# Experts of a decoder trunk: weights as the loaded operand, blocks of 96 token rows streamed beside their rests

## The chip, the cores and the metric

The kernel runs on one core of a Trainium2 chip. The metric is the device time of one execution in microseconds (us). TensorE (PE in the profile, with its weight loads as PEld), VectorE (DVE), ScalarE (ACT), GpSimd (POOL) and the DMA queue of SyncE (SP) run side by side and are ordered by semaphores alone.

## The reference, cut to what matters

One inference step of a two-layer trunk for 256 prompt rows and 32 sample rows (T = 288), width D = 1024. Layer 0 is a Mamba and attention mixer with a dense SwiGLU; layer 1 is RWKV-7 time mixing and a mixture of 8 experts, of which each row goes to 2. The change is in the experts:

```python
def _swiglu(h, wg, wu, wd):
    return (jax.nn.silu(h @ wg) * (h @ wu)) @ wd
...
    logits = jnp.einsum('bld,de->ble', h.astype(f32), router.astype(f32))
    top_v, top_i = lax.top_k(logits, TOP_K)
    gates = jax.nn.softmax(top_v, axis=-1)
...
    for e in range(N_EXPERTS):
        y = y + combine[..., e:e + 1] * _swiglu(h, wg[e], wu[e], wd[e]).astype(f32)
```

`wg` and `wu` are 1024 x 2816 and `wd` is 2816 x 1024 for each expert, in float32: 34.6 MB an expert.

## The kernel before, in words

Every expert product is made in fp32r, a faster 32-bit form of TensorE with fewer mantissa bits. To keep the precision each operand is split in a head (the value rounded to fp32r) and a rest (value less head, rounded), and three products are added: head by head, head by rest, rest by head. For the weights ACT makes the heads (`heads`, lines 1411 to 1423) and DVE the rests (`rests`, lines 2138 to 2150).

Token rows are first grouped: each expert's rows go into a block of 128 slots, and an expert with more rows than slots gets a further block. A block is a *job*. DVE works out the number of jobs on the chip (`jobf`, `jobi`, `jobs_ready`); the engines run job 0, a loop over the middle jobs and the last job, which is expert 7. Job 0's rows are picked by matmuls; those of later jobs come from a DRAM scratch `moe_rows`, fetched by POOL (`next_rows`) and turned by TensorE into `hsel` (`turn_tokens`, line 3080). After a job ACT copies the result to `ysb` (`rows_out`), and POOL stores it in `moe_back` (`store_rows`, waiting for the landing). In the last job the rows of the other experts are gathered (`pair`, `DMA_INDIRECT`), scaled, turned (`pair_turn`) and added to `x`; the last expert's own rows are put back by a matmul with `sel_last`.

In a job the 2816 hidden units go in FC = 11 chunks of 256. SP loads a chunk's weights in two DMAs, gate and up (2 MB, "gu") and down (1 MB, "dn"), into one of MS = 4 slots; a slot's part is loaded again when its matmuls are done (`gu_slot_free`, `dn_slot_free`). TensorE's order in a job is written out by hand:

```python
                for c in range(FC + 2):
                    if c < FC:
                        up(c)
                    if c >= 2:
                        down(c - 2)
                    if 1 <= c < FC:
                        turn(c - 1)
```

`up(c)` makes gate and up of 256 units for 128 token rows in one PSUM bank. For each of 8 k tiles the token columns are loaded and 512 weight columns are streamed, three times (every matmul is issued in the helper at line 2342):

```python
                        mm(ps[:, c % 2, :], hh[:, k, :], wh[:, k, :], k == 0, False)
                        mm(ps[:, c % 2, :], hh[:, k, :], wr[:, k, :], False, False)
                        ins = mm(ps[:, c % 2, :], hr[:, k, :], wh[:, k, :], False, k == KT - 1)
```

Then ACT takes silu of the gate half (line 1486), DVE multiplies by the up half (line 2291), TensorE turns the product by two transposes (`turn`, line 3127), ACT makes its head (line 1493) and DVE its rest (line 2307). `down(c)` loads these (128 units by 128 rows) and streams 512 columns of the down weights, 12 matmuls. One chunk's heads and rests are in the queues of ACT and DVE between these steps, two chunks ahead of TensorE.

Of the kernel before, what the change touches and what calls it, by code (L numbers as in the profile page):

```python
# [32 lines left out]
FC = FF // 256  # L33
C_DECAY = float(np.exp(-0.5))
# [95 lines left out]
def decoder_trunk(nc, a, out):  # L130
    with ExitStack() as ctx:
# [216 lines left out]
        sgm = moe_area(256)  # L348
        actm = [moe_area(256) for _ in range(2)]

        actTm = [[actTm_[:, (2 * i + u) * 256:(2 * i + u + 1) * 256] for u in range(2)] for i in range(2)]
# [6 lines left out]
        NJ = NE + 4  # L358
        flags, posn, erow, jrow = [moe_area(16) for _ in range(4)]
        ohx, tmpx = [moe_area(64).rearrange("p (x i) -> p x i", x=4) for _ in range(2)]  # L360
# [11 lines left out]
        DOWN_BANKS = [0, 1, 2, 7, 5, 6, 3, 4]  # L372
        moe_rows = nc.dram_tensor("moe_rows", ((NJ + 1) * P, D), F32, kind="Internal").ap()
        moe_back = nc.dram_tensor("moe_back", (NJ * P, D), F32, kind="Internal").ap()

# [13 lines left out]
        def turned(c):  # L389

            return ps[:, 2 if c % 2 == 0 else 7, 0:256]
# [368 lines left out]
        def _(sp):  # L760
# [110 lines left out]
            jl = sp.value_load(jobi[0:1, 4:5], min_val=NE - 1, max_val=NJ - 1)  # L871
# [12 lines left out]
        def _(pool):  # L884
# [15 lines left out]
            for n, t in enumerate(X_ORDER):  # L900
# [11 lines left out]
                if n == 4:  # L912
                    pool.wait_ge(sem("pool_cleared"), 2)
                    pool.dma_start(moe_rows.rearrange("(b p) n -> p b n", p=P), zeros.unsqueeze(1).broadcast_to([P, NJ + 1, D]))\
                        .then_inc(sem("rows_zeroed"), 16)
                    pool.dma_start(moe_back[(NE - 1) * P:, :].rearrange("(b p) n -> p b n", p=P),
                                   zeros.unsqueeze(1).broadcast_to([P, NJ - NE + 1, D])).then_inc(sem("rows_zeroed"), 16)
# [91 lines left out]
            jl = pool.value_load(jobi[0:1, 4:5], min_val=NE - 1, max_val=NJ - 1)  # L1009
            def next_rows(j):  # L1010
                pool.wait_ge(sem("gather_full"), 2 * j + 2)
                pool.dma_start(xtok, moe_rows[bass.ds(j * P + P, P), :]).then_inc(sem("xtok_loaded"), 16)
# [7 lines left out]
            next_rows(0)  # L1020
            with pool.Fori(1, jl) as j:
                next_rows(j)
                store_rows(j)
            pool.wait_ge(sem("gather_full"), 2 * jl + 2)
            store_rows(jl)
            for c, (t0, n) in enumerate(TOK):
                if c == 2:
                    pool.wait_ge(sem("pair_summed"), 1)
                    pool.wait_ge(sem("y_final"), 2)
                for a_ in range(2):  # L1030
                    pool.indirect_dma_start(pair[a_][c][0:n, :], None, moe_back,
                                            bass.IndirectOffsetOnAxis(ap=rows_in[0:n, 3 * a_ + c:3 * a_ + c + 1], axis=0))\
                        .then_inc(sem(f"pair_loaded{c}"), 16)


        @block.scalar
        def _(act):
# [387 lines left out]
            def token_heads(j, u):  # L1425

                act.wait_ge(sem("gather_full"), 2 * j + 1 + u)
                A(hsel[0][:, 4 * u:4 * u + 4, :], ps[:, 5 + u, :].rearrange("p (k c) -> p k c", k=4), ACT.Copy)\
                    .then_inc(sem("hsel_head"), 1)

            def rows_out(j):
# [3 lines left out]
                A(ysb[:, 0:512], ps[:, 3, :], ACT.Copy)  # L1435
                A(ysb[:, 512:1024], ps[:, 4, :], ACT.Copy).then_inc(sem("y_out"), 1)
# [29 lines left out]
            def job(j, first, last=False):  # L1466
# [4 lines left out]
                else:  # L1471
                    heads(j, 0, "gu", range(4))
                    rows_out(j)
                    heads(j, 1, "gu", range(2))
                for c in range(FC + 1):
# [858 lines left out]
        def _(pe):  # L2334
# [748 lines left out]
            def job(j, opening, last=False):  # L3083
# [67 lines left out]
                for c in range(FC + 2):  # L3151
# [4 lines left out]
                    if 1 <= c < FC:  # L3156
                        turn(c - 1)
# [125 lines left out]
```

## Time and profile before

| | |
|---|---|
| median of 3 runs | 1634.34 us (1631.61 to 1641.16) |
| profiled execution | 1637.31 us |
| its span, first to last instruction | 1634.3 us |
| mean granted TensorE clock, share of 2.4 GHz | 0.987 |
| PE, PEld, DVE, ACT, POOL busy, share of the span | 97%, 80%, 70%, 55%, 8% |

All stretches and waits below are of the profiled execution. Busy time of an engine is the time that at least one of its instructions is running; matmuls are pipelined, so a matmul's own duration is longer than the distance to the next one. A granted clock of 1.00 is 2.4 GHz, 0.50 is 1.2 GHz. The experts begin at about 850 us; before that come the mixers and the dense layer.

### The profile page before, as it was taken

The page shows a single profiled execution, that of the slowest core. Times are in us where ns is not written, and L with a number is a line of the kernel's source. Part 1 is how long each engine was busy: PE and PEld are TensorE (multiplying, and loading weights), DVE is VectorE, ACT ScalarE, POOL GpSimd, SP SyncE. Part 2 cuts the span into 40 slices and gives each one's busy share as a digit, 9 for nine tenths or more (in the row PEclk, how much of TensorE's full clock was granted, in tenths as well). Part 3 has the DMA queues.
Part 4 walks back from the last instruction along what each step waited for, and adds up shares of the span by engine and source line. Part 5 has one row for each costly group of instructions (what it writes and reads, how often), then busy time and mean ns, then how long its engine had stood idle before and what let it go on. Part 6 is the DMA issues. An engine that isn't in the chain of part 4 may idle for free.

```text
span 1634.3 us, 27320 instructions
## 1 busy us (share of the span) xinstructions
PE 1590.1 (97%) x10856; PEld 1309.2 (80%) x10856; DVE 1137.9 (70%) x1476; ACT 896.8 (55%) x1190; POOL 123.3 (8%) x180
## 2 busy tenths in 40 slices
PE   9999999999999999899999999999999999999999
PEld 7766687999998777778767878888787887878787
DVE  4663741677766753335468889797988979798897
ACT  3362541544325353343436777676777767687774
POOL 1104000000000003220222000000000000000100
PEclk9999889999999999998999999999999999999999
DMA  8923533544423240000449999797989979798993
GB/s 334 407 94 124 207 130 123 220 187 170 175 81 119 103 155 1 3 3 2 187 165 395 380 376 412 316 427 305 425 350 376 409 312 426 303 425 347 384 423 121
DMA packets 41103, 404.74 MB, mean 248 GB/s; under 512 B 4784, under 2 KB 5072, under 8 KB 11664
## 3 DMA queue, kind: packets, MB, share of 16 engines
q1 hardware_dynamic: 34336, 372.25, 56.6%
q0 software_dynamic: 6672, 31.14, 4.7%
q8 instruction: 70, 1.15, 0.3%
q14 instruction: 25, 0.20, 0.0%
HBM read 379.09 MB, written 26.30 MB: 248 GB/s over the span
## 4 chain that ended last, share of the span: by engine, by line
PE 88%; DVE 5%; ACT 2%; DMA 2%; issue 2%; POOL 0%; DVEq 0%; ACTq 0%; SPq 0%; POOLq 0%
PE ps L2342 85%; DMA ring<-in_moe_w 1%; PE ps L3127 1%; DMA arena<-in_moe_w 1%; DVE rest_ring L2149 1%; PE ps L2809 1%; PE ps L2750 1%; DVE arena L1688 0%; ACT arena L1270 0%; DVE arena L1701 0%; ACT arena L1283 0%; PE ps L3080 0%; PE ps L2544 0%; DVE h L2057 0%; DVE arena L1776 0%
## 5 line engine op out<-in xcount | busy, mean ns | idle before, releaser
L2342 PE MATMUL ps<-head,hsel 128*128 128x512 f32 x1408 | 457.5, 396 | 2.8 <-DVE rest_ring L2149 2.8
L2342 PEld LDWEIGHTS ps<-head,hsel 128*128 128x128 f32 x1408 | 264.3, 188 | 61.5 <-DVE rest_ring L2149 7.8
L2149 DVE TENSOR_TENSOR rest_ring<-ring,head 128x2048 fp32r<-128x2048 f32 x128 | 291.0, 2284 | 14.4 <-ACT head L1423 14.3
L2342 PE MATMUL ps<-arena,ring 128*128 128x288 f32 (+9 forms) x1408 | 256.6, 347 | 1.3 <-ACT arena L1276 1.2
L1423 ACT ACTIVATE head<-ring 128x2048 fp32r<-128x2048 f32 x128 | 243.1, 1912 | 24.9 <-DMA ring<-in_moe_w 24.9
L2342 PEld LDWEIGHTS ps<-arena,ring 128*128 128x128 f32 (+4 forms) x1408 | 199.5, 189 | 53.1 <-issue 7.7
L2342 PE MATMUL ps<-rest_ring,hsel 128*128 128x512 f32 x512 | 199.6, 390 | 0.0
L2342 PE MATMUL ps<-head,actT_split 128*128 128x512 f32 x512 | 169.1, 394 | 9.0 <-issue 6.3
L2342 PE MATMUL ps<-rest_arena,head 128*128 128x288 f32 x704 | 174.8, 296 | 0.0
L2342 PE MATMUL ps<-rest_arena,rest_ring 128*128 128x288 f32 x528 | 155.5, 294 | 0.0
L2342 PE MATMUL ps<-h,ring 128*128 128x288 f32 (+2 forms) x624 | 133.6, 370 | 3.7 <-ACT h L1332 1.9
L2342 PEld LDWEIGHTS ps<-h,ring 128*128 128x128 f32 (+2 forms) x624 | 99.6, 176 | 37.6 <-issue 10.7
L2342 PEld LDWEIGHTS ps<-head,actT_split 128*128 128x128 f32 x512 | 96.1, 188 | 33.3 <-issue 9.1
L2342 PEld LDWEIGHTS ps<-rest_arena,head 128*128 128x128 f32 x704 | 122.5, 188 | 0.1
L2143 DVE TENSOR_TENSOR rest_ring<-ring,head 128x2048 fp32r<-128x2048 f32 x48 | 109.7, 2285 | 9.7 <-ACT head L1418 9.7
L2149 DVE TENSOR_TENSOR rest_arena<-arena,head 128x1024 fp32r<-128x1024 f32 (+1 forms) x64 | 110.3, 1750 | 3.7 <-ACT head L1423 3.5
L2342 PEld LDWEIGHTS ps<-rest_ring,hsel 128*128 128x128 f32 x512 | 96.4, 188 | 18.0
L2342 PE MATMUL ps<-arena 64*64 64x64 f32 (+13 forms) x1514 | 96.9, 266 | 9.9 <-DVE arena L1721 4.0
L2342 PE MATMUL ps<-hsel,head 128*128 128x288 f32 x352 | 103.8, 295 | 0.0
L1599 DVE TENSOR_TENSOR x<-x,ps 128x288 f32<-128x288 f32 x110 | 48.2, 452 | 77.6 <-PE ps L2342 77.3
L1423 ACT ACTIVATE head<-arena 128x1024 fp32r<-128x1024 f32 (+1 forms) x64 | 92.4, 1485 | 15.9 <-DMA arena<-in_moe_w 15.6
L2342 PE MATMUL ps<-rest_ring,actT_split 128*128 128x512 f32 x256 | 99.7, 389 | 0.0
(387 smaller groups left out, 2283.1 us busy)
## 6 DMA issues: line engine op xcount, KB each, us to landing
ring<-in_moe_w SPq DMA_DIRECT2D x64, 2048.0 KB, 12.4
ring<-in_moe_w SPq DMA_DIRECT2D x64, 1024.0 KB, 8.3
arena<-in_moe_w SPq DMA_DIRECT2D x24, 2048.0 KB, 11.6
arena<-in_moe_w SPq DMA_DIRECT2D x24, 1024.0 KB, 6.6
ring<-in_ffn_w SPq DMA_DIRECT2D x11, 2048.0 KB, 7.4
ring<-in_ffn_w SPq DMA_DIRECT2D x11, 1024.0 KB, 4.8
moe_rows<-arena POOLq DMA_DIRECT2D x1, 6656.0 KB, 34.0
ring<-in_w_in SPq DMA_DIRECT2D x2, 3072.0 KB, 12.8
```

The costliest lines, as they stand in the source:

```text
L1423: A(mhead[c % 2][:, o:o + w], mslot[s][:, o:o + w], ACT.Copy).then_inc(sem("gu_head"), 1)
L1599: V.tensor_tensor(x[:, m, :], x[:, m, :], bank(g)[:, 0:T], ALU.add).then_inc(freesem(g), 1)
L2143: V.tensor_tensor(mrest[s][:, GU:SLOT], mslot[s][:, GU:SLOT], down_head(c).bitcast(F32), ALU.subtract).then_inc(sem("dn_split"), 1)
L2149: V.tensor_tensor(mrest[s][:, o:o + w], mslot[s][:, o:o + w], mhead[c % 2][:, o:o + w].bitcast(F32), ALU.subtract).then_inc(sem("gu_split" ...
L2342: return nc.tensor.matmul(o, l, r, start=start, stop=stop, skip_group_check=skip)
L2750: ins = nc.tensor.transpose(b[0:rows, i * P:(i + 1) * P], src[:, 4 * hf + i, t0:t0 + rows], ident)
L2809: ins = nc.tensor.transpose(b[:, n * P:(n + 1) * P], Mi[gg % 2][:, h0:h0 + 2, :].rearrange("p h t -> p (h t)"), ident)
L3127: ins = nc.tensor.transpose(turned(c)[:, u * P:(u + 1) * P], actm[c % 2][:, u * P:(u + 1) * P], ident)
```

## The change

- Blocks have 96 slots (`SL`), not 128; thresholds, row numbers, scratch tensors and the number of possible further blocks (5, not 4) follow.
- In `up` the weights are the loaded operand and token rows are streamed. Head and rest of the token rows stand beside each other in `hsel` (192 columns), so head by head and rest by head are one matmul; the third, with the rests of the weights, streams the 96 head columns. 64 matmuls a chunk. The result has hidden units on partitions: two banks, in each two 128-unit blocks with (head columns, rest columns).
- The two parts are summed: ACT copies the rest columns (`gsum`), DVE adds the head columns (`act_sums`). Then silu (ACT, now from SBUF), product (POOL), head (ACT), rest (POOL). `turn` is gone; the token transposes have 96 columns.
- POOL's queue now has, per job, the products and rests of 11 chunks (`activations`), and between them the store of the last job's rows (after chunk 0), the wait for its landing (after chunk 1), and in the last job the gathers (after chunks 1 and 7).
- `down` loads 96 columns in place of 128. PSUM banks: 0 and 1, 2 and 3 for gate and up; 4 and 5 for down; 6 and 7 for token rows. ACT makes the first head piece of the next job before its last activation head.

```diff
+SL = 96
-        hsel = [hsel_[:, i * 1024:(i + 1) * 1024].rearrange("p (k c) -> p k c", k=KT) for i in range(2)]
+        hsel = hsel_[:, 0:2 * KT * SL].rearrange("p (k a c) -> p k a c", k=KT, a=2)
-        NJ = NE + 4
+        NJ = NE + 5
...
+        def gu_banks(c):
+
+            b = GU_BANKS[c % 2]
+            return ps[:, b:b + 2, 0:4 * SL].rearrange("p b (i a s) -> p b i a s", i=2, a=2)
...
-            def store_rows(j):
-                pool.wait_ge(sem("y_out"), j)
-                pool.dma_start(moe_back[bass.ds(j * P - P, P), :], ysb).then_inc(sem("back_stored"), 16)
-                pool.wait_ge(sem("back_stored"), 16 * j)
-                pool.sem_inc(sem("ysb_free"), 1)
+            def activations(j, first, c):
+
+                if c or not first:
+                    pool.wait_ge(sem("moe_act_rest"), FC * j + c)
+                pool.wait_ge(sem("sums_then_silu"), 2 * FC * j + 2 * c + 2)
+                nc.gpsimd.tensor_tensor(actm, sgm[c % 2], gsum[c % 2][:, 2 * SL:4 * SL], ALU.mult).then_inc(sem("actm_ready"), 1)
+                pool.wait_ge(sem("moe_act_head"), FC * j + c + 1)
+                nc.gpsimd.tensor_tensor(actTm[c % 2][1], actm, actTm[c % 2][0].bitcast(F32), ALU.subtract)\
+                    .then_inc(sem("moe_act_rest"), 1)
+            def job(j, first, last=False):
+                if not last:
+                    next_rows(j)
+                for c in range(FC):
+                    activations(j, first, c)
+                    if c == 0 and not first:
+                        pool.wait_ge(sem("y_out"), j)
+                        pool.dma_start(moe_back[bass.ds(j * SL - SL, SL), :], ysb[0:SL]).then_inc(sem("back_stored"), 16)
+                    if c == 1 and not first:
+                        pool.wait_ge(sem("back_stored"), 16 * j)
+                        pool.wait_ge(sem("gather_full"), 2 * j + 2)
+                        pool.sem_inc(sem("ysb_free"), 1)
+                    if last and c == 1:
+                        pair_rows(0)
+                        pair_rows(1)
...
+            def act_silu(j, c):
+
+                act.wait_ge(sem("gu_free"), FC * j + c + 3)
+                A(sgm[c % 2], gsum[c % 2][:, 0:2 * SL], ACT.Silu).then_inc(sem("sums_then_silu"), 1)
+            def act_head(j, c):
+
+                act.wait_ge(sem("actm_ready"), FC * j + c + 1)
+                if c >= 2:
+                    act.wait_ge(sem(f"dn_slot_free{(c - 2) % MS}"), uses[(c - 2) % MS] * j + (c - 2) // MS + 2)
+                A(actTm[c % 2][0], actm, ACT.Copy).then_inc(sem("moe_act_head"), 1)
...
+                    A(sums4(c), gu_banks(c)[:, :, :, 1, :], ACT.Copy).then_inc(sem("sums_then_silu"), 1)
...
+                    act_silu(j, c)
                     if c + 2 < FC:
                         heads(j, c + 2, "gu", range(1, 2))
+                    if c == FC - 1 and not last:
+                        heads(j + 1, 0, "gu", range(0, 1))
+                    act_head(j, c)
...
+            def act_sums(j, c):
+
+                dve.wait_ge(sem("sums_then_silu"), 2 * FC * j + 2 * c + 1)
+                V.tensor_tensor(sums4(c), gu_banks(c)[:, :, :, 0, :], sums4(c), ALU.add).then_inc(sem("gu_free"), 1)
...
-                        mm(ps[:, c % 2, :], hh[:, k, :], wh[:, k, :], k == 0, False)
-                        mm(ps[:, c % 2, :], hh[:, k, :], wr[:, k, :], False, False)
-                        ins = mm(ps[:, c % 2, :], hr[:, k, :], wh[:, k, :], False, k == KT - 1)
+                        for i in range(4):
+                            cols_ = slice(i * P, (i + 1) * P)
+                            both = sums[:, i // 2, i % 2]
+                            if k == KT - 1:
+                                mm(both[:, 0], wr[:, k, cols_], hsel[:, k, 0, :], False, False, skip=True)
+                            ins = mm(both, wh[:, k, cols_], hsel[:, k], k == 0 and i % 2 == 0, k == KT - 1, skip=True)
+                            if k < KT - 1:
+                                mm(both[:, 0], wr[:, k, cols_], hsel[:, k, 0, :], False, False, skip=True)
...
-                    for u in range(2):
-                        ins = nc.tensor.transpose(turned(c)[:, u * P:(u + 1) * P], actm[c % 2][:, u * P:(u + 1) * P], ident)
...
-                        mm(ps[:, 3 + hf, :], ah[:, us], wh[:, u, cols_], begins, False)
+                        mm(ps[0:SL, DOWN + hf, :], ah[:, us], wh[:, u, cols_], begins, False)
```

## Rows read from the trace of the kernel before

**Rows 1.** The page: busy us (share of the span) x instructions; costliest group.
```profile
PE 1590.1 (97%) x10856; PEld 1309.2 (80%) x10856; DVE 1137.9 (70%) x1476; ACT 896.8 (55%) x1190; POOL 123.3 (8%) x180
...
L2342 PE MATMUL ps<-head,hsel 128*128 128x512 f32 x1408 | 457.5, 396 | 2.8 <-DVE rest_ring L2149 2.8
```

**Rows 2.** The chain of waits that ended last, shares of the span by engine.
```profile
PE 88%; DVE 5%; ACT 2%; DMA 2%; issue 2%; POOL 0%; DVEq 0%; ACTq 0%; SPq 0%; POOLq 0%
```

**Rows 3.** Two stretches: us, PE, PEld, DVE, ACT, POOL busy (x), PEclk, DMA share, GB/s.
```profile
949.39:1044.96 95.57, 94.41 (x427) 76.93 (x428) 82.53 (x60) 70.24 (x62) 1.10 (x2) 1.00 0.91 374
...
1523.32:1634.27 110.95, 106.32 (x485) 85.91 (x485) 96.56 (x86) 73.61 (x66) 12.12 (x7) 1.00 0.75 310
```

**Rows 4.** The chain in order of time, one job's end and start: start, us, what.
```profile
1235.16 0.87 PE ps L3080 x8
...
1259.04 1.58 issue
...
1263.63 0.22 PE ps L3127 x2
1263.85 8.17 PE ps L2342 x36
...
1280.66 8.20 PE ps L2342 x36
```

**Rows 5.** Timeline at a job's start, TensorE idle before: start us, us, engine, line.
```profile
1154.72 0.19 PEld L2342 LDWEIGHTS ps<-head,hsel 128*128 128x128 f32 x1 [0.82 <-DVE rest_ring L2149]
1154.72 0.50 PE L2342 MATMUL ps<-head,hsel 128*128 128x512 f32 x1 [0.40 <-DVE rest_ring L2149]
1154.83 0.19 PEld L2342 LDWEIGHTS ps<-rest_ring,hsel 128*128 128x128 f32 x1
1155.06 0.40 PE L2342 MATMUL ps<-rest_ring,hsel 128*128 128x512 f32 x1
```

**Rows 6.** Timeline, weight loads in the time mixer, plain fp32, 64 columns streamed each.
```profile
776.62 0.86 PEld L2342 LDWEIGHTS ps<-arena,ring 128*128 128x128 f32 x7 [0.24 <-issue]
```

**Rows 7.** Timeline, fp32r matmuls of 288 columns in the dense layer.
```profile
442.83 0.29 PE L2342 MATMUL ps<-rest_arena,rest_ring 128*128 128x288 f32 x1
442.96 0.42 PE L2342 MATMUL ps<-rest_arena,head 128*128 128x288 f32 x2
```

**Rows 8.** Groups by form, six jobs (949.39 to 1523.32): busy us, mean ns, idle before.
```profile
L2149 DVE TENSOR_TENSOR rest_ring<-ring,head 128x2048 fp32r<-128x2048 f32 x96 | 218.2, 2284 | 3.7 <-ACT head L1423 3.6
L2342 PEld LDWEIGHTS ps<-head,hsel 128*128 128x128 f32 x1056 | 198.2, 188 | 46.9 <-DVE rest_ring L2149 6.7
L1423 ACT ACTIVATE head<-ring 128x2048 fp32r<-128x2048 f32 x96 | 182.3, 1912 | 10.8 <-DMA ring<-in_moe_w 10.8
...
L2149 DVE TENSOR_TENSOR rest_arena<-arena,head 128x1024 fp32r<-128x1024 f32 x24 | 27.7, 1217 | 0.0
L2291 DVE TENSOR_TENSOR moe<-moe,ps 128x256 f32<-128x256 f32 x66 | 27.7, 419 | 51.2 <-ACT moe L1486 51.1
...
L1486 ACT ACTIVATE moe<-ps 128x256 f32<-128x256 f32 x66 | 25.3, 384 | 90.2 <-PE ps L2342 90.2
...
L3127 PEld LDWEIGHTS ps<-cst,moe 128*128 128x128 f32 x132 | 18.0, 139 | 7.8
...
L2156 DVE TENSOR_TENSOR hsel<-ps,hsel 128x512 fp32r<-128x512 f32 x12 | 7.7, 682 | 0.0
```

**Rows 9.** One line of POOL, both operands in SBUF: duration ns min/median/max.
```profile
L954 POOL TENSOR_TENSOR ring<-ring,cst x40: 632/635/1180, 629.1 to 738.2; 128x256 f32<-128x256 f32 x40
```

**Rows 10.** One line of DVE, both operands in SBUF: duration ns min/median/max.
```profile
L1543 DVE TENSOR_TENSOR arena<-arena x21: 451/452/736, 271.3 to 842.8; 128x288 f32<-128x288 f32 x21
```

**Rows 11.** Busy time in a stretch of the time mixer (columns as in rows 3).
```profile
640.00:660.00 20.00, 16.68 (x448) 13.15 (x446) 8.82 (x17) 13.13 (x32) 4.57 (x8) 1.00 0.01 3
```

**Rows 12.** DMA issues in six jobs: KB each, median us from issue to landing.
```profile
moe_back<-moe POOLq DMA_DIRECT2D x6, 512.0 KB, 10.2
```

More of the change, by code:

```diff
@@ L357, in decoder_trunk @@
         rows_in = moe_area(6).bitcast(U32)
-        NJ = NE + 4
+        NJ = NE + 5
         flags, posn, erow, jrow = [moe_area(16) for _ in range(4)]
-        ohx, tmpx = [moe_area(64).rearrange("p (x i) -> p x i", x=4) for _ in range(2)]
+        ohx, tmpx = [moe_area(80).rearrange("p (x i) -> p x i", x=5) for _ in range(2)]
         rk = moe_area(32)
@@ L1033, in _ @@
                         .then_inc(sem(f"pair_loaded{c}"), 16)
+            def job(j, first, last=False):
[13 more added lines that the diff above has]
+                        pair_rows(1)
+                    if last and c == 7:
+                        pool.wait_ge(sem("pair_summed"), 1)
+                        pool.wait_ge(sem("y_final"), 2)
+                        pair_rows(2)
+            job(0, True)
+            with pool.Fori(1, jl) as j:
+                job(j, False)
+            job(jl, False, last=True)
         @block.scalar
@@ L2284, in job @@
                     rests(j, 0, "gu", range(4))
-                    rests(j, 1, "gu", range(0, 1))
-                for c in range(FC + 1):
-                    if c < FC:
-                        dve.wait_ge(sem("silu_ready"), FC * j + c + 1)
-                        if c >= 2:
-                            dve.wait_ge(sem("tr_full"), FC * j + c - 1)
-                        V.tensor_tensor(actm[c % 2], sgm, ps[:, c % 2, 256:512], ALU.mult).then_inc(sem("gu_free"), 1)
+                    rests(j, 1, "gu", range(2))
+                for c in range(FC):
+                    act_sums(j, c)
                     if last and c in (2, 3):
@@ L2297, in job @@
                         pair_add(j, c // 2 - 3, c % 2)
-                    if c == 0 and not first:
-                        rests(j, 1, "gu", range(1, 2))
-                    if 1 <= c <= FC - 2:
+                    if c:
                         rests(j, c - 1, "dn", range(1))
                     if c + 2 < FC:
-                        rests(j, c + 2, "gu", range(0, 1))
-                    if c:
-                        dve.wait_ge(sem("tr_head"), FC * j + c)
-                        hd = actTm[(c - 1) % 2]
-                        V.tensor_tensor(hd[1], turned(c - 1), hd[0].bitcast(F32), ALU.subtract).then_inc(sem("tr_free"), 1)
-                    if c + 2 < FC:
-                        rests(j, c + 2, "gu", range(1, 2))
-                    if c == FC - 2:
-                        rests(j, c, "dn", range(1))
+                        rests(j, c + 2, "gu", range(2))
                 rests(j, FC - 1, "dn", range(1))
```

154 lines of the change are left out of this document (67 added, 87 removed).

## The prediction

> **What bounds the kernel now.** I read the page's busy times first: PE is busy 97% of the span, DVE 70%, ACT 55%, POOL 8%, and the experts' gate and up matmuls are the costliest group, 1408 records; they are two of the three matmuls of each k tile, so one job has 11 x 8 x 2 = 176 of them and there are 8 jobs [rows 1]. The chain of waits gives PE 88% [rows 2]. Busy PE is no proof of peak speed, so I went to the stretch by job: a full job takes 95.6 us, PE is busy for 94.4 of it at granted clock 1.00, DVE 82.5, ACT 70.2, DMA engines 91% of the time; the last one takes 110.95 with its tail [rows 3]. The chain inside a job then says what the job is made of: 36 matmuls in 8.17 to 8.20 us, two transposes in 0.22 us, eleven times; eight transposes of token rows in 0.87 us once; and a few short waits at the job's start [rows 4]. So one matmul of 512 streamed columns costs 8.20 / 36 = 0.228 us from start to start. 512 columns at 2.4 GHz are 0.213 us. TensorE's order of work sets the end and the other engines follow: whatever changes TensorE's time for one chunk is paid 88 times.
>
> The jobs stay eight. A block of 96 rows would need a further job for each expert with over 96 rows, but the reference's router, evaluated on the reference's inputs, gives the eight experts 70, 77, 68, 84, 76, 64, 60 and 77 rows.
>
> **The change part by part.**
>
> *Gate and up matmuls.* Before, a chunk of 256 hidden units takes 8 k tiles x 3 matmuls = 24, each loading 128 token columns and streaming 512 weight columns: 24 x 0.228 = 5.47 us. After, the weights are loaded: 8 k tiles x 4 column blocks x 2 = 64 matmuls, each loading 128 x 128, half of them streaming 192 columns (heads beside rests) and half 96. By columns that is 32 x (192 + 96) = 9216 in place of 12288. If only columns counted, this would be a gain. So the question is what a weight load costs when little is streamed behind it.
>
> The trace answers twice. When TensorE has been idle and an fp32r matmul starts, its load starts at 1154.72, the next load at 1154.83 and the second matmul at 1155.06 [rows 5]: 0.34 us from first to second start in place of 0.228. The extra 0.11 is the first load standing alone, and the next load begins when it is over. So a 128 x 128 fp32r load takes 0.11 us before its matmul can stream; with 512 columns behind it that is hidden. The second place has loads of 128 columns with only 64 streamed: seven loads in 0.86 us, and the last one's own record is 0.19, so starts are (0.86 - 0.19) / 6 = 0.112 us apart [rows 6]. These are plain fp32, which streams each column twice: the streaming alone would be 0.053. There the load is the bound, at clock 1.00 as in the experts.
>
> 192 columns are 0.080 us and 96 are 0.040, both under 0.11, so all 64 starts should be a load apart. No row shows fp32r with few streamed columns. Bounds: below, 0.108, the bare load of rows 5; above, 0.120, since fp32r matmuls have a fixed part over their columns that plain ones lack (288 columns, 0.120 us, start 0.13 apart [rows 7]; 512 have 0.015), which might add to the load. I take 0.112, the row that is bound in the same way. Up costs 64 x 0.112 = 7.17 us (6.91 to 7.68), 1.70 more.
>
> Here a page speaks otherwise. The Trainium skill, TensorE: Matmul & The Clock Gate, section Back-to-back issue gap, gives about 81 ns for each sustained pair of load and 128-column matmul. By it up would be 64 x 0.081 = 5.18 us, a gain; no run here shows 0.081, and rows 5 and 6 show more, so I don't use it in the sum.
>
> *Transposes of activations.* They go: two per chunk, 0.22 us [rows 4]. Gate and up now come out with hidden units on partitions.
>
> *Down matmuls.* 12 per chunk, 512 streamed, as before: 12 x 0.228 = 2.74. Their load has 96 columns, hidden as 128 were. Token transposes: at most the same 0.87 per job.
>
> *A chunk.* Before 8.20 + 0.22 = 8.42 (11 of them and 0.87 leave 2.1 of a job of 95.6 for waits). After 7.17 + 2.74 = 9.91, 1.49 more.
>
> *The evacuation chain.* It now has six steps: ACT copies the products with token rests (384 elements), DVE adds, ACT silu (192), POOL multiplies, ACT makes the head, POOL the rest. The old steps took 0.38 to 0.42 us for 256 elements and 0.68 (DVE) for 512 [rows 8], so 384 on DVE is 0.55. ACT per chunk: three heads of 1.91, plus about 0.5, 0.3 and 0.3: 6.8 us. DVE: three rests of 2.28 plus 0.55: 7.4 us, against 7.7 before. POOL: two operations of some 0.6 us (635 ns for 256 elements, with one operand broadcast [rows 9]; here 192). All below 9.91: hidden. down(c) stands after up(c+2), 2 x (7.17 + 2.74) = 19.8 us behind up(c)'s end, and the chain with two heads of ACT work between needs about 6 to 8. At the job's end down(10) follows up(10) by down(8), the token transposes and down(9), 6.3 us: nearly tight, since POOL's two steps can each stand behind one of DVE's 2.28 us instructions.
>
> *POOL against DVE.* POOL's operation of 635 ns takes up to 1180, DVE's of 452 up to 736 [rows 9, 10], each with both operands in SBUF and where the other engine works on SBUF too. So DVE may lose 2 x 0.28 to 2 x 0.54 us a chunk: 8.0 to 8.5. Still under 9.91; with a faster TensorE it would not be.
>
> *Moved waits.* POOL's store of rows and its landing (10.2 us [rows 12]) now stand between its products at c = 0 and c = 1; next in its queue are the products of chunk 2, which ACT's head waits for, and behind that ACT's heads of weights. down(2) starts 19.8 us after up(2), so nothing is late. In the last job four indirect gathers stand there too; the same slack covers them if they hold POOL for under some 10 us. Loads from DRAM: same bytes at a slower pace, 91% of 95.6 in 110. Their queue waits for slots freed by the same matmuls. What is left at a job's start is the DVE piece for up(0); I leave 0.5 us of waits, because pieces of 1.22 us on DVE now feed 1.79 us of matmuls.
>
> *Sum.* A job: 11 x 9.91 + 0.87 + 0.5 = 110.4, against 95.6: 14.8 more, x 8 = 118. The last job's PE idles 4.6 us against 1.2 in a full one [rows 3]; those 3.4 should vanish, as weights come early enough now. +115. Router, mixers and dense layer are untouched. The profiled execution took 1637.31 us (span 1634.3); with the change 1752. The median of the runs is 1634.34: 1749.
>
> **Rivals.**
>
> *Loads are cheaper than that and columns count (faster).* The place is the same 64 matmuls. For it: transposes' loads of 128 columns have a record of 139 ns where the fp32r ones have 188 [rows 8]. If the load took 49 ns less, 192 columns would cost 0.093 and 96 some 0.054 to 0.067: up 4.7 to 5.15, a chunk 7.4 to 7.9, and then DVE at 8.0 to 8.5 becomes the bound. Job 89 to 94.5, mid value 91: 4.6 x 8 = 37 less, 1597. It decides when the mean interval is under (8.42 - 2.74) / 64 = 0.089 us. Against it: the 0.11 of rows 5 is on fp32r loads themselves. The Trainium skill, SBUF — State Buffer, section Who interferes with whom, says that a two-SBUF-input DVE instruction and a POOL one that reads SBUF exclude each other; by this rule the gain would stop at DVE as reckoned, and the trace agrees (452 to 736 ns, rows 10).
>
> *The load isn't hidden at all when streams are short:* 0.108 + 0.080 and 0.108 + 0.040, with fixed parts about 0.17 on average: up 10.9, chunk 13.6, +5.2 x 88 = +458, less 12 of waits: 2080. Against it: in rows 6 load and stream overlap (0.112, not 0.16).
>
> *The granted clock falls to 1.2 GHz in the experts,* since TensorE streams only half of the time there. A chunk doubles to 19.8: +1000, 2630. Against it: the stretch of small products with PE gaps of 17% stays at 1.00 [rows 11].
>
> **How the numbers follow.** Load bound, slower: 0.83. Cheaper loads: 0.08. Unhidden loads 0.04, clock 0.03, other 0.02. Time 1749, the likeliest. Its range: interval 0.108 gives -23, 0.120 gives +45; waits of 0 to 2.5 a job give -4 to +16; the last job's stall kept +3. That is 1722 to 1813; I trim the corner where all are high and take 1718 to 1805, which leaves out the rivals. Faster by over 0.5% 0.08, within 0.5% (what a measurement of this kernel can't tell from none) 0.01, slower 0.91.
>
> **What the profile after would show.** PE's expert matmuls of 192 and 96 columns start 0.108 to 0.120 us apart whatever their width; PEld is then continuous; up about 7.2 us, chunk about 9.9, job about 110; DVE and ACT each idle 1.5 to 3 us a chunk; DMA share near 0.8; clock 1.00. I am wrong if the two widths differ in interval (loads not the bound), if DVE rests or POOL products end TensorE's waits, if a granted clock of 0.5 stands in the expert stretch, or if there are more than eight jobs.

## The result, and the profile after

The median went from 1633.47 us (1631.61 to 1641.16) to 1898.15 us (1896.36 to 1899.15): ratio 1.161, 95% interval 1.158 to 1.165. Forecast were 1749 us and 1718 to 1805. The direction and the first mechanism were right, but the forecast is 149 us low.

The page after; columns as in [rows 1, 2]:

```profile
PE 1841.3 (97%) x14200; PEld 1617.9 (85%) x14200; DVE 1172.5 (62%) x1388; ACT 918.6 (48%) x1278; POOL 383.9 (20%) x356
...
PE 85%; DVE 6%; issue 5%; ACT 2%; POOL 1%; DMA 0%; DVEq 0%; POOLq 0%; ACTq 0%
...
L2373 PE MATMUL ps<-hsel,head 128*128 128x192 f32 (+1 forms) x3168 | 855.1, 345 | 18.4 <-issue 18.3
L2190 DVE TENSOR_TENSOR rest_ring<-ring,head 128x2048 fp32r<-128x2048 f32 x128 | 327.7, 2599 | 14.6 <-ACT head L1454 14.6
```

PE is as busy as before, 97%. That alone would pass for "TensorE does more work". The issue share in front of the new matmuls (18.3 us) is the first hint that something else has come in. Then the stretches by job, with the columns of [rows 3]: job 1 up to its last downs, the first 44 us of job 2, and the rest of job 2:

```profile
988.49:1092.82 104.33, 104.23 (x821) 96.71 (x820) 81.25 (x44) 67.39 (x66) 31.92 (x22) 1.00 0.82 321
1102.90:1147.20 44.30, 44.13 (x200) 42.84 (x199) 18.05 (x11) 15.83 (x16) 8.13 (x6) 0.50 0.57 223
1147.20:1236.00 88.80, 87.04 (x645) 77.69 (x644) 66.66 (x38) 55.60 (x55) 25.57 (x19) 1.00 0.73 281
```

PE is busy in all three, but in the second at granted clock 0.50 (1.2 GHz), with 200 matmuls in 44 us. Six such stretches stand in the experts, one at the opening of each of jobs 0 and 2 to 6; jobs 1 and 7 have none. The weight loads of up, at full clock and then in such a stretch (timeline, PEld):

```profile
1150.02 0.19 PEld L2373 LDWEIGHTS ps<-hsel,rest_ring 128*128 128x128 f32 x1
1150.13 0.19 PEld L2373 LDWEIGHTS ps<-hsel,head 128*128 128x128 f32 x1
1150.24 0.19 PEld L2373 LDWEIGHTS ps<-hsel,rest_ring 128*128 128x128 f32 x1
```

```profile
1110.08 0.33 PEld L2373 LDWEIGHTS ps<-hsel,head 128*128 128x128 f32 x1
1110.29 0.33 PEld L2373 LDWEIGHTS ps<-hsel,rest_arena 128*128 128x128 f32 x1
```

They start 0.111 us apart at full clock and 0.21 at half, the same for both widths. The starts of the matmuls themselves alternate (timeline, PE):

```profile
1149.73 0.32 PE L2373 MATMUL ps<-hsel,head 128*128 128x192 f32 x1
1149.88 0.23 PE L2373 MATMUL ps<-hsel,rest_ring 128*128 128x96 f32 x1
1149.95 0.32 PE L2373 MATMUL ps<-hsel,head 128*128 128x192 f32 x1
```

The next one starts 0.156 us behind one of 192 columns and 0.067 behind one of 96. Taken by itself that is a sign of being wrong that the prediction names (the two widths differ), but a pair always takes 0.223 us, two loads, so the pace is that of the loads. At full clock up takes 7.12 us, down 2.78, a chunk 9.90. Last, the end of job 2 and the start of job 3 (timeline; DVE's first weight rests, PE's last down, PE's first up):

```profile
1231.67 4.62 DVE L2190 TENSOR_TENSOR rest_arena<-arena,head 128x1024 fp32r<-128x1024 f32 x4
...
1233.95 0.40 PE L2373 MATMUL ps<-head,actT_split 128*96 128x512 f32 x1
...
1237.92 0.35 PE L2373 MATMUL ps<-hsel,head 128*128 128x192 f32 x1 [3.57 <-issue]
```

The first of the four rests was done at 1232.9, both pieces of hsel before it. No engine's work is late here, and yet for 3.57 us TensorE runs nothing. The trace's record of its branch at the end of the loop's body begins at 1231.5 and lasts 6.04 us. The five branches that go back take 5.9 to 6.3 us, and 0.22 to 0.24 in the kernel before; the sixth, which leaves the loop, 0.08. The instruction queue q8 moved 125 packets (2.05 MB), against 70 (1.15 MB): TensorE's body has 844 matmuls, each with a load, in place of 426.

So my account of the miss, from the starts of matmuls: from down(9) to the next up(0) five times 3.8 us more than in jobs that follow no branch (19 us); and the three opening ups at 41.0 to 41.3 us in place of 21.4, with the first down at 3.5 to 5.0 in place of 2.8, six times (127 us). Together 146. (The experts take 147 us more than the sum said, as counted below; the small rest of the 149 lies ahead of them.)

### The profile page after: what moved, and what is told of

It reads as the page before. It is cut to its first block, busy times and chain, and to the rows that moved or that the text cites. A ratio compares the mean times of both kernels' runs of the same rounds, so it can differ in the third digit from the quotient of the medians.

```text
span 1894.7 us, 34341 instructions
## 1 busy us (share of the span) xinstructions
PE 1841.3 (97%) x14200; PEld 1617.9 (85%) x14200; DVE 1172.5 (62%) x1388; ACT 918.6 (48%) x1278; POOL 383.9 (20%) x356
## 3 DMA queue, kind: packets, MB, share of 16 engines
q8 instruction: 125, 2.05, 0.4%
## 4 chain that ended last, share of the span: by engine, by line
PE 85%; DVE 6%; issue 5%; ACT 2%; POOL 1%; DMA 0%; DVEq 0%; POOLq 0%; ACTq 0%
PE ps L2373 84%; DVE rest_ring L2184 1%; DVE rest_arena L2190 1%; PE ps L2840 1%; POOL moe L1028 1%; DMA moe_back<-moe 0%; PE ps L2781 0%; DVE arena L1729 0%; ACT arena L1301 0%; DVE arena L1742 0%; ACT arena L1314 0%; PE ps L2575 0%; DVE h L2098 0%; DVE arena L1817 0%; POOL actT_split L1030 0%
## 5 line engine op out<-in xcount | busy, mean ns | idle before, releaser
L2373 PE MATMUL ps<-hsel,head 128*128 128x192 f32 (+1 forms) x3168 | 855.1, 345 | 18.4 <-issue 18.3
L2373 PEld LDWEIGHTS ps<-hsel,head 128*128 128x128 f32 x3168 | 684.0, 216 | 25.3 <-issue 20.8
L2373 PE MATMUL ps<-hsel,rest_ring 128*128 128x96 f32 x2048 | 493.4, 251 | 0.0
L2373 PEld LDWEIGHTS ps<-hsel,rest_ring 128*128 128x128 f32 x2048 | 441.6, 218 | 2.1
L2190 DVE TENSOR_TENSOR rest_ring<-ring,head 128x2048 fp32r<-128x2048 f32 x128 | 327.7, 2599 | 14.6 <-ACT head L1454 14.6
L1028 POOL TENSOR_TENSOR moe<-moe 128x192 f32<-128x192 f32 x88 | 125.4, 1425 | 637.3 <-ACT moe L1472 637.3
L2373 PE MATMUL ps<-hsel,rest_arena 128*128 128x96 f32 x768 | 189.5, 257 | 1.7 <-issue 1.7
L2373 PE MATMUL ps<-head,actT_split 128*96 128x512 f32 x512 | 178.0, 410 | 1.4 <-DVE rest_ring L2184 0.7
L2373 PEld LDWEIGHTS ps<-hsel,rest_arena 128*128 128x128 f32 x768 | 170.5, 225 | 3.1 <-issue 2.4
L1030 POOL TENSOR_TENSOR actT_split<-moe,actT_split 128x192 fp32r<-128x192 f32 x88 | 142.6, 1621 | 70.5 <-ACT actT_split L1479 70.5
L2373 PEld LDWEIGHTS ps<-h,ring 128*128 128x128 f32 (+2 forms) x624 | 99.5, 176 | 37.4 <-issue 10.5
L2373 PEld LDWEIGHTS ps<-head,actT_split 128*96 128x96 f32 x512 | 86.6, 169 | 39.9 <-POOL actT_split L1030 3.5
```

What stands on the lines that cost most here:

```text
L1028: nc.gpsimd.tensor_tensor(actm, sgm[c % 2], gsum[c % 2][:, 2 * SL:4 * SL], ALU.mult).then_inc(sem("actm_ready"), 1)
L1030: nc.gpsimd.tensor_tensor(actTm[c % 2][1], actm, actTm[c % 2][0].bitcast(F32), ALU.subtract)\
L2190: V.tensor_tensor(mrest[s][:, o:o + w], mslot[s][:, o:o + w], mhead[c % 2][:, o:o + w].bitcast(F32), ALU.subtract).then_inc(sem("gu_split" ...
L2373: return nc.tensor.matmul(o, l, r, start=start, stop=stop, skip_group_check=skip)
```

## The experiments

The theory: the branch leaves TensorE idle, the granted clock falls, and three ups with thin streams in a row don't bring it back; the first wide matmuls (down(0)) do. Rivals: thin streams alone bring it down; the idle time comes from DVE or GpSimd; the fall has a length of its own.

Times up to job 0's first up differ by up to 13 us between runs of kernels that are alike there (852 to 865 us), so beside each median stands the *experts' part*, from the start of that matmul to the end in the profiled execution: 776.0 us before, 1037.5 after. The prediction's sum was 776 + 115 = 891. "On e1" means that the edit is made in the first experiment's kernel, which has no branch on TensorE between jobs; its time is 1771 us.

**TensorE's middle jobs written out.** (e1)

```diff
-            with pe.Fori(1, jl) as j:
+            for j in range(1, NE - 1):
                 job(j, False)
```

> TensorE's middle jobs of the changed kernel are written out one after the other in place of its loop; every other engine keeps its loop. Theory (an idle time of TensorE at the loop's branch lets the granted clock fall, and the three ups that follow without a down hold it down): the five idle times of 3.8 us go (19 us), and with them the falls at the openings of jobs 2 to 6 (21.2 us each, 106); the fall in job 0, which has no branch before it, stays. 1898 - 19 - 106 = 1773 us. Rival 1 (thin streams alone bring the clock down wherever three ups follow each other): only the idle times go, 1879. Rival 2 (the idle time is not the branch but late pieces from DVE or POOL): no change, 1898.

Measured 1771.45 us, ratio 1.082 (1.077 to 1.088); experts' part 912.5. One row of windows, the three opening ups of job 2:

```profile
1093.11:1114.52 21.41, 21.41 (x193) 21.41 (x192) 18.27 (x11) 15.91 (x16) 7.85 (x5) 1.00 1.00 394
```

No idle time, clock 1.00, 21.4 us. Three thin ups in a row don't bring the clock down by themselves (rival 1 would be 1879). Five of the six falls went with the branch; job 0's stayed.

**The idle time put back without a branch** (on e1; e5)

```diff
                 if not first:
+                    for n_ in range(2):
+                        V.reduce_sum(tmpx[:, n_, 0:KT], x, AX)
                     rests(j, 0, "gu", range(4))
```

> The kernel of the run with TensorE's jobs written out (1771 us), with DVE made late: before its first weight rest of each job but the first it sums all of x twice (about 2.4 us each, result not used), so that up(0) waits some 3.4 us for DVE (2 to 5) although there is no branch. Theory (any idle time of TensorE in front of three thin ups brings the clock down, the branch is only one maker of it): falls of about 44 us at the openings of jobs 1 to 7, 21 us each: 1771 + 7 x (3.4 + 21) = 1942 us. Rival (the fall needs what comes with the branch, such as the fetch of instructions): no falls, 1771 + 7 x 3.4 = 1795 us.

Measured 1945.03 us, ratio 1.184 (1.179 to 1.189); experts' part 1079.8. DVE and PE at the start of job 3 (timeline), and that opening (windows):

```profile
1259.02 5.00 DVE L2330 TENSOR_REDUCE moe<-x 128x8 f32<-128x2304 f32 x2
1263.94 4.61 DVE L2190 TENSOR_TENSOR rest_arena<-arena,head 128x1024 fp32r<-128x1024 f32 x4
...
1265.25 0.33 PE L2375 MATMUL ps<-hsel,head 128*128 128x192 f32 x1 [3.58 <-issue]
```

```profile
1265.25:1305.68 40.43, 40.43 (x192) 40.43 (x193) 21.11 (x12) 12.90 (x12) 7.82 (x5) 0.51 0.64 247
```

The view calls this idle time issue too, though here it ends when DVE's first piece does: the label alone tells no cause. All seven openings behind such a wait now run at half clock, those of jobs 1 and 7 as well. An idle time of 3.6 us was enough here; the branch is only what made it in the changed kernel.

**The branch moved in front of down(9) and down(10)** (loop kept; e6; down(9)'s waits for its operands move to the end of the body, ahead of the branch)

```diff
             def job(j, opening, last=False):
...
+                if not opening:
+                    down(FC - 2, True)
+                    down(FC - 1, True)
-                for c in range(FC + 2):
+                for c in range(FC + 2 if last else FC):
```

> The changed kernel with its loop, but the turn of the loop on TensorE is moved: down(9) and down(10) of a job stand after the branch, ahead of the next job's up(0). Instructions and their order on every engine are the same. Theory: the idle time at the branch stays (five times 3.8 us), but 24 wide matmuls follow it, so the clock is back before the three ups; falls of some 3.4 us as in the kernel before with two jobs a turn, under 2 us each; job 0 keeps its fall. 1771 + 19 + 8 = 1798 us. Rival (an idle time brings a long fall whatever follows): 1898.

Measured 1823.7 us, ratio 1.111 (1.106 to 1.117); experts' part 959.5, 47 more than in e1. The first matmul behind the branch, and the windows of the two downs and of the three ups behind them:

```profile
1217.75 0.71 PE L2373 MATMUL ps<-head,actT_split 128*96 128x512 f32 x1 [7.11 <-issue]
```

```profile
1217.75:1225.89 8.14, 8.14 (x24) 5.48 (x25) 5.33 (x3) 0.98 (x1) 0.00 (x0) 0.66 0.56 168
1225.89:1247.31 21.42, 21.42 (x193) 21.41 (x192) 11.78 (x7) 13.88 (x14) 7.85 (x5) 1.00 0.97 387
```

The clock fell here too, but the wide streams brought it back within the two downs, which took 8.1 us in place of 5.8, and the ups ran at full clock. So what follows the idle time sets the price: 2.3 us or 21. I was 26 us low. The idle time grew from 3.8 us to 6.9 to 7.1, 15 us in five turns; the downs lost 4 us more than I had counted; the other 7 us are within what the stages ahead of the experts vary by. In the loop as it was, the 12 queued matmuls of down(10) ran on for 2.8 us behind the branch's start; here only eight short transposes stood in front of the branch.

**12 wide matmuls inside up(0) and up(1)** (loop kept; e2)

```diff
+                        if k == KT - 1 and c < 2:
+                            for n_ in range(12):
+                                mm(ps[0:SL, TOKB + n_ % 2, :], hsel[:, n_ % 8, 0, :], wh[:, n_ % 8, :])
                         for i in range(4):
```

> The changed kernel, loop kept, with 12 matmuls of 512 columns into banks that nobody reads before the last k tile of up(0) and of up(1) in every job. At full clock they cost 2 x 2.74 = 5.5 us a job. Theory (the clock comes back once wide streams run, whatever they compute): up(0) still runs at half clock, and the clock comes back within the first wide matmuls, so an affected opening costs about 7 + 2 us in place of 21; 1898 - 6 x 12 + 8 x 5.5 = 1870 us. Rival (the fall has a fixed length of some 44 us whatever TensorE streams): 12 wide ones at half clock cost 5.5 each time, 11 a job; 1898 + 6 x 11 + 2 x 5.5 = 1975. The idle time at the branch stays at 3.8 us in both.

Measured 1885.1 us, ratio 1.150 (1.144 to 1.156); experts' part 1022.3. The falls are shorter (windows at job 3: up(0) with its wide matmuls, then what follows):

```profile
1236.40:1256.90 20.50, 15.79 (x65) 14.56 (x66) 2.34 (x2) 0.00 (x0) 0.00 (x0) 0.50 0.52 207
1256.90:1275.60 18.70, 18.70 (x152) 17.59 (x151) 11.77 (x7) 12.92 (x12) 7.84 (x5) 1.00 0.78 300
```

The fall has no length of its own (1975 is excluded): it ended with the wide matmuls of up(0). The falls cost 6.2 to 7.6 us an opening (26.9 us at full clock), less than the 9 I had counted. The gain is smaller than expected for another reason: behind each branch TensorE stands still a second time, in up(0) after five matmuls (timeline):

```profile
1237.22 0.49 PE L2373 MATMUL ps<-hsel,head 128*128 128x192 f32 x1
1242.41 0.24 PE L2373 MATMUL ps<-hsel,rest_arena 128*128 128x96 f32 x1 [4.70 <-issue]
```

These five idle times of 4.6 to 5.4 us, 25 us together, have no match in the other runs; in the one shown DVE's four pieces for up(0) had ended at 1234.3. The edit makes TensorE's body longer (868 matmuls), but why it stops there is not shown.

**The kernel before, two jobs in each turn of TensorE's loop** (e3)

```diff
-            with pe.Fori(1, jl) as j:
-                job(j, False)
+            with pe.Fori(0, NE // 2 - 1) as i_:
+                job(2 * i_ + 1, False)
+                job(2 * i_ + 2, False)
```

> The kernel before, with two jobs in each turn of TensorE's loop (three turns in place of six), so that the loop's body has about as many instructions (some 850 matmuls) as the changed kernel's body has. Theory (a taken branch costs TensorE some 6 us once the body is this long, whatever the streams; and wide streams bring the clock back soon): two back edges with a branch of about 6 us and an idle time of 3 to 4 us, three job starts without a branch; a clock fall, if any, of under 6 us each. 1634 + 2 x 3 - 3 x 1.6 = 1635 us, up to 1645 with short clock falls. Rival (the long branch comes from narrow matmuls or from the other engines' state in the changed kernel, not from the body's length): branches stay at about 0.2 us, 1629 to 1634.

Measured 1651.05 us, ratio 1.010 (1.003 to 1.017); experts' part 791.3, 15.3 more. That is over my 1635 to 1645 us, and well over the rival's 1629 to 1634. Its two branches back take 6.7 and 6.2 us. The first matmul behind one (timeline) and the opening ups (windows):

```profile
1153.50 0.64 PE L2342 MATMUL ps<-head,hsel 128*128 128x512 f32 x1 [4.08 <-issue]
```

```profile
1153.50:1167.02 13.52, 12.95 (x48) 10.13 (x49) 6.74 (x5) 6.43 (x5) 0.00 (x0) 0.87 1.01 423
```

The long branch comes from the length of the body, not from the new matmuls. The clock fell here as well, and cost 1.8 us (13.5 in place of 11.75) with 512 columns streamed at once. About the same idle time costs some 20 us with thin streams. The two branches and their falls make 11.5 of the 15.3 us; the rest are longer waits in front of the first down of some jobs and changes too small to place. Behind one of these, of 1.8 us and without a branch, the clock fell too, for 3.4 us (windows, job 2's up(2) and down(0)):

```profile
1063.11:1074.95 11.84, 10.01 (x40) 7.67 (x39) 10.91 (x8) 8.01 (x7) 0.00 (x0) 0.87 1.02 434
```

Behind an idle time of 1.9 us that ended at 974.0 in the same run it didn't fall. So no least idle time for a fall can be read from these runs.

**The kernel before, TensorE's jobs written out** (the edit of e1; e4)

> The kernel before with TensorE's middle jobs written out in place of its loop. Theory: the idle 1.58 us marked as issue at each of five back edges goes, 8 us: 1626 us. Rival (what TensorE waits for there is DVE's first piece, so the branch is covered): 1634.

Measured 1637.01 us, ratio 1.002 (0.999 to 1.006): no change, the rival's time. The branch of 0.23 us was covered, and the waits marked issue [rows 4] stay.

**Job 0: wide matmuls ahead of it** (on e1; e7)

```diff
+            def wide(n):
+                pe.wait_ge(sem("gu_head"), 1)
+                for n_ in range(n):
+                    mm(ps[:, DOWN + n_ % 2, :], mhead[0][:, 0:P], mhead[0][:, 0:512])
+
+            wide(8)
             pe.wait_ge(sem("pick_ready"), 1)
...
             pick_tokens(0)
+            wide(8)
             pick_tokens(1)
+            wide(8)
```

> The kernel with TensorE's jobs written out (1771 us), with 24 matmuls of 512 columns, whose results are not used, around the two products that pick job 0's tokens: 8 while TensorE waits for the picks, 8 between, 8 behind. They cost 5.5 us less the 1.2 us idle that they fill. Theory: the fall at job 0's opening goes like those of the other jobs: 1771 - 21 + 4 = 1754 us, and the prediction's model of 1749 is reached. Rival (job 0's fall has another cause than the thin and broken work ahead of it): 1775.

The fall at job 0 needs a test of its own, since no idle time of 3.6 us stands ahead of it. In e1 (timeline) the longest is 1.23 us, and then come the 48 thin matmuls that pick the tokens; at the same place in the kernel before (48 matmuls of 128 columns, then 512 at once) the clock stayed at 1.00.

```profile
843.56 8.09 PE L2373 MATMUL ps<-arena 128*128 128x96 f32 x48 [1.23 <-ACT arena L1497]
```

Measured 1766.09 us, ratio 1.075 (1.070 to 1.079), between my 1754 and the rival's 1775; experts' part 902.0 (the wide matmuls stand ahead of it and are not in it). The opening's long fall went; which of the 24 did it, and what exactly makes the clock fall there, is not shown. But a new idle time stood at down(0), with a short fall behind it. PE's and ACT's waits from 845 to 900 (sum, times, longest) and the chain there:

```profile
ACT actT_split L1479 <- POOL moe L1028: 12.8, 1, 12.8
...
PE ps L2373 <- DVE rest_arena L2184: 8.6, 1, 8.6
```

```profile
872.34 12.11 DMA moe_rows<-arena,moe
...
886.84 0.61 POOL moe L1028
887.50 0.24 issue
887.74 1.89 ACT head L1449
...
890.60 2.21 DVE rest_arena L2184
892.81 0.14 issue
892.95 7.06 PE ps L2373 x33
```

POOL makes product 0 only when its scatter of token rows has landed. ACT's activation head waits for it, and behind that in ACT's queue the down head, then DVE's rest, then down(0). In the kernel after, ACT waits there too (11.3 us), but the slow clock gave the time.

**GpSimd: three chunks of job 0 ahead of that landing** (on e7; e9; GpSimd's wait for the job list moves behind job 0)

```diff
-            pool.wait_ge(sem("rows_scattered"), 96)
-            pool.sem_inc(sem("ysb_free"), 1)
...
                     activations(j, first, c)
+                    if first and c == 2:
+                        pool.wait_ge(sem("rows_scattered"), 96)
+                        pool.sem_inc(sem("ysb_free"), 1)
+                        next_rows(j)
```

> The run with 24 wide matmuls ahead of job 0 (1766 us), and GpSimd's products and rests of job 0's chunks 0 to 2 are put ahead of its wait for the scattered rows to land and of its wait for the job list. In the run before GpSimd came to the product of chunk 0 only after that landing (12.1 us) and TensorE idled 8.6 us at down(0), and a fall of 10.2 us followed. Theory (this wait is a second cost of the change, which the fall of the clock in job 0 had covered): the idle time and the fall go, 8.6 + 5 us less: 1752 us, the model of the prediction (1749) plus 4 us of wide matmuls. Rival (down(0) in job 0 waits for the weights' heads and rests, not for GpSimd): 1766.

Measured 1763.1 us (1751.94 to 1766.16), ratio 1.077 (1.071 to 1.083). By the median alone nothing was gained. But the stage ahead took 5 us longer in this run (up(0) starts at 868.0, 862.8 in the last one), and whether by the edit or by chance is not shown. The experts' part is 891.3 us: the 8.6 us of idle time and the short fall are gone. The opening of job 0:

```profile
867.96:889.37 21.41, 21.41 (x193) 21.41 (x192) 15.52 (x31) 12.80 (x12) 12.60 (x10) 1.00 0.99 404
```

**Half the streamed columns of one product** (on e1; e8)

```diff
-                                mm(both[:, 0], wr[:, k, cols_], hsel[:, k, 0, :], False, False, skip=True)
+                                mm(both[:, 0, 0:SL // 2], wr[:, k, cols_], hsel[:, k, 0, 0:SL // 2], False, False, skip=True)
```

> The kernel with TensorE's jobs written out (1771 us), where the products with the weights' rests stream 48 columns in place of 96 (the other 48 get no such product). Theory (each start waits for a load of 128 columns, whatever is streamed): intervals stay 0.112 us, up 7.12 us, 1771 us, as long as the granted clock holds. Rival 1 (columns count with the load): 32 x 0.020 us less in each chunk, 88 x 0.64 = 56 us less, 1715. Rival 2 (the clock needs streamed columns: with a sixth fewer it falls in the middle of jobs too): up to 2400 us.

Measured 1772.14 us, ratio 1.078 (1.074 to 1.083); experts' part 913.6. Its loads start 0.11 us apart as before:

```profile
1139.85 0.19 PEld L2373 LDWEIGHTS ps<-hsel,rest_arena 128*128 128x128 f32 x1
1139.96 0.19 PEld L2373 LDWEIGHTS ps<-hsel,head 128*128 128x128 f32 x1
1140.07 0.19 PEld L2373 LDWEIGHTS ps<-hsel,rest_arena 128*128 128x128 f32 x1
```

The matmuls' starts now alternate by 0.172 and 0.051 us, 0.223 a pair as before. So the columns cost nothing behind a load here, and a sixth fewer of them don't bring a full clock down.

**Activations on DVE** (on e1; e10: the two `nc.gpsimd.tensor_tensor` of `activations` become `V.tensor_tensor`, the product between the two gate and up rests, the rest behind them; two rests of the last job stay on GpSimd)

> The kernel with TensorE's jobs written out (1771 us), with the products and rests of activations on DVE in place of GpSimd (two rests of the last job stay on GpSimd); DVE then has about 8.0 us of work in a chunk of 9.9. Theory (TensorE is bound by its loads; GpSimd is off its path in all chunks but those of job 0, where the clock's fall covers it): 1771 us, within 5. Rival (DVE's weight rests, lengthened from 2284 to 2599 ns by GpSimd, or GpSimd's own steps of 1.4 and 1.6 us, hold TensorE up somewhere): 1750 to 1760.

Measured 1778.41 us (1774.11 to 1782.26), ratio 1.088 (1.083 to 1.093); experts' part 910.7, 1.8 less than e1. The median lies 7 us over e1's, outside my 5; the profiled execution's first up started 10 us later (862.2 against 851.8), so the difference in the medians isn't the experts'. DVE by form, jobs 1 to 6:

```profile
L2190 DVE TENSOR_TENSOR rest_ring<-ring,head 128x2048 fp32r<-128x2048 f32 x96 | 218.7, 2283 | 7.5 <-ACT head L1454 7.5
...
L2335 DVE TENSOR_TENSOR moe<-moe 128x192 f32<-128x192 f32 x65 | 22.8, 351 | 0.0
```

A weight rest takes 2283 ns, 2599 beside GpSimd, whose product takes 1425 ns where DVE needs 351. That is real contention, and worth nothing while the loads bound TensorE.

**Half the loads** (on e1; e11: the `wr` product left out of `up`; 32 matmuls are left)

> The kernel with TensorE's jobs written out (1771 us), with the 32 products of the weights' rests left out of each up (less precise: rest by head is missing). All DVE, ACT, GpSimd and DMA work stays. Theory (the loads alone set TensorE's pace): up has 32 loads, 3.58 us, and down 2.78, 6.36 a chunk, which is under what DVE (7.4 to 8.4 us with GpSimd beside it) and the loads from memory (3.1 MB at 374 GB/s, 8.4 us) need, so a chunk takes 8.0 to 8.8 us: 1771 - 88 x 1.5 = 1640 us (1600 to 1680), as fast as the kernel before at best, unless TensorE's waits bring its clock down, which then costs up to 3.6 us a chunk and ends near 1771 again. Rival (loads are not the bound, streamed columns are: a third fewer): 88 x (32 x 0.040) = 113 us less, 1658, with TensorE never idle.

Measured 1621.71 us, ratio 0.989 (0.983 to 0.995). Half a millisecond of its experts (windows):

```profile
1000.00:1500.00 500.00, 422.18 (x2734) 351.50 (x2734) 480.21 (x265) 405.42 (x397) 237.07 (x133) 0.99 0.96 394
```

A chunk takes 7.87 us (from the starts of its matmuls), with DVE busy 96% and the DMA engines 96%: a bit below my 8.0 to 8.8. TensorE waits in each chunk, and the clock hardly suffers there (0.99), perhaps since a down is never far. Job 0's down(0) is the exception: it comes 31.2 us behind the first up against 15.1 in job 1, and 16.5 of these TensorE is idle for the late rest that the wide matmuls ahead of job 0 had laid bare (e7). So the expectation of the next run puts down to the clock what is mostly this wait. Where these 32 matmuls of 192 columns don't wait (up(3) of job 0), they take 3.55 us, 0.111 each. The column rival falls: it wanted 1658 with TensorE never idle.

**The same product left out of the kernel before** (e12)

```diff
-                        mm(ps[:, c % 2, :], hh[:, k, :], wr[:, k, :], False, False)
```

> The kernel before, with the product of token heads and weight rests left out of gate and up, the same product that the run with half the loads leaves out (less precise in the same way). TensorE then has 16 x 0.228 + 0.22 + 2.74 = 6.6 us in a chunk, 0.25 us more than the other orientation (6.36). Theory (with the third product gone both orientations are bound by DVE and the weights' DMA, at 7.7 to 7.9 us a chunk, and the orientation earns nothing): 1636 - 88 x 0.6 = 1583 us, 1570 to 1600; faster than the 1622 of the other orientation, which lost some 20 us to a low clock in job 0 and more to its longer chain of steps. Rival (the new orientation is the better one once its loads are halved): over 1622.

Measured 1570.36 us, ratio 0.958 (0.952 to 0.964), at the low end of my 1570 to 1600 and 51 us under the other orientation. The stretch in its experts:

```profile
950.00:1450.00 500.00, 451.69 (x1946) 351.67 (x1944) 477.36 (x340) 402.10 (x351) 5.94 (x11) 0.98 0.99 414
```

So the new orientation is no gain with two products either, even with the 16 us of job 0 taken off. Both of these compute with less precision; no version with all three products beat the kernel before.

## Why the prediction was right and wrong

- **Load bound: right.** Forecast interval 0.112, up 7.17, down 2.74, chunk 9.91, job 110.4 us. Measured in jobs at full clock: 0.111, 7.12, 2.78, 9.90, and 110.2 in e1. The halved stream (e8) and the halved loads (e11) show the cause. The Trainium skill's 81 ns for a pair (TensorE: Matmul & The Clock Gate, section Back-to-back issue gap) does not show in the expert matmuls, whose mean interval is 0.111 us with 192, 96 or 48 columns.
- **Transposes, down, eight jobs: right.** With all openings at full clock and hardly a wait the experts' part is 891.3 us, and the prediction's sum is 891. That they agree to 0.3 us is luck, as the next point shows.
- **The last job's stall: wrong.** The sum takes off 3.4 us of idle time, "as weights come early enough now". But 3.0 of the 4.6 us stand behind TensorE's last matmul (1631.3 of 1634.3), where the other engines finish, and they stay. TensorE is idle 4.6 us in the last job before and 3.7 after, and the job grew by 14.8 us, not by 11.4. The other seven grew by 100.5 us together (in e9), where the sum has 103.6. The two errors of 3 us cancel. The last job, kernel before and after (windows):

```profile
1528.74:1634.27 105.53, 100.90 (x462) 81.46 (x460) 91.14 (x81) 69.14 (x60) 12.12 (x7) 1.00 0.74 306
1774.41:1894.75 120.34, 116.68 (x880) 105.14 (x878) 93.36 (x69) 71.04 (x71) 54.52 (x29) 1.00 0.67 268
```

- **The step that failed: "What is left at a job's start is the DVE piece for up(0); I leave 0.5 us of waits".** The sum had no term for TensorE's branch. Only DVE's and ACT's readiness was looked at; the doubled count of TensorE's instructions was not. Measured: 3.8 us at five job starts, 19 us; e1 removed them, and e3 made them in the kernel before by the length of the body alone.
- **With it fell the dismissal of "The granted clock falls to 1.2 GHz in the experts".** I had priced that rival as all or nothing (2630 us) and argued against it from [rows 11], a stretch that stays at 1.00 with 17% of gaps. That says nothing of what follows one longer idle time. Measured: 127 us in six openings; a clock of 0.5 in the expert stretch was one of the prediction's own signs of being wrong. For the five behind a branch e1, e5 and e6 show both halves: an idle time of some 3.6 us took the clock down, and thin streams left it down until wide ones came. In job 0 wide matmuls ahead of it kept it up (e7). The Trainium skill (TensorE: Matmul & The Clock Gate, section Loop structure matters more than you think) says that a long wait turns the clock down and that dense work keeps it up. The trace agrees with the first (0.50 behind 3.6 us of idle time), and e1 with the second (1.00 throughout its middle jobs); but PE was busy through the opening ups in the kernel after and stayed at 0.50. What exactly decides this is not settled here.
- **GpSimd hidden: right in jobs 1 to 7, wrong in job 0,** where its product stood behind a scatter's landing. Its two operations were also under-sized: some 0.6 us each in the forecast, 1.4 and 1.6 measured; in jobs 1 to 7 the slack hid it. The slow clock covered the wait in job 0; once it was gone, the wait and the fall behind it cost 10.7 us (902.0 to 891.3).
- **The columns rival's next bound:** DVE was to stop the chunk at 8.0 to 8.5 us. With half the loads it came to 7.87, with DVE and DMA both at 96%.

The 146.5 us between 1037.5 and 891.0: 125.0 by writing TensorE's jobs out, 10.5 by the wide matmuls ahead of job 0, 10.7 by GpSimd's order; 0.3 are left. The wide matmuls' own time stands ahead of the experts and is not in this account.

## What to carry to other kernels

Before making the small operand the streamed one, count weight loads: a 128-column load cost 0.11 us here, and streams of 96 and 48 columns behind it were free but gained nothing. When an edit multiplies an engine's instructions inside a loop, price the branch back as well, and look at what stands behind each idle time of TensorE: here wide streams brought the clock back for some 2 us, and thin ones ran at half speed for 40. And a slow stretch hides waits; when it is mended, expect the next one.

## What was not expected of the hardware

- A branch back on TensorE took 0.22 to 0.24 us with 426 matmuls in the body, and 5.9 to 6.7 us with 844 or 852. Matmuls already queued run on during it (2.8 us of them here). The branches of ACT, DVE and GpSimd in the changed kernel have records of 0.04 to 0.07 us.
- At half clock weight loads slow down too: 0.21 us apart in place of 0.111.
- With PE busy 100% and loads back to back, the granted clock stayed at 0.50 for 41 us, and the same 192 matmuls kept a clock of 1.00 once they began with it. The lengths of the falls differ by what follows: 41 to 55 us with three thin ups, 10 in e6, 3.4 in e3.
